# State-space rounds of a hybrid encoder: the step-weighted inputs made by ScalarE head by head, GpSimd making only the rows of the end states

## What is computed

```
acs  = cumsum(dt * A)                       # within a chunk of 128
xdt  = x * dt                               # the inputs weighted with the step size
Lm   = exp(acs[t] - acs[s]) for s <= t
y_diag = (C B^T * Lm) @ xdt                 # within a chunk
states = B^T @ (exp(acs_end - acs) * xdt)   # what a chunk adds to the state
prev   = scan of states over the chunks
y      = y_diag + (C @ prev) * exp(acs)
```

## Time and profile before

| | |
|---|---|
| median of 3 runs | 2319.83 us (2319.46 to 2322.78) |
| profiled execution | 2323.43 us, its span 2321.9 us |
| mean granted TensorE clock | 0.990 |
| busy: PE, DVE, ACT, POOL | 97%, 63%, 44%, 16% |
| state-space rounds | about 630 to 980 us of the span |
| `xdt` on POOL (L2349) | 48 instructions, 37.2 us, 801 ns in the mean |
| waits of POOL for PE ahead of `xdt` | 253.2 us |
| `rl` on ACT (L1287) | 192 instructions, 57.8 us |

### The profile page before, as it was taken

The page is one execution under the profiler, slowest core; times in us unless marked ns, Lnnn a source line. Parts: engine busy times, 40 slices in busy tenths (PEclk is TensorE's granted clock), DMA queues, the critical chain, the costliest instruction groups (busy, mean ns, idle before and its releaser), DMA issues.

```text
span 2321.9 us, 36382 instructions
## 1 busy us (share of the span) xinstructions
PE 2259.2 (97%) x13148; PEld 2013.1 (87%) x13148; DVE 1462.5 (63%) x2345; ACT 1016.0 (44%) x1651; POOL 371.1 (16%) x257
## 2 busy tenths in 40 slices
PE   8999999998999999999999999999999999999997
PEld 7999999997877777888888888888888899899996
DVE  7677677678778888422555555542246677677677
ACT  6334243344444754632455655544235334243244
POOL 2000000000012202133333333322333000000000
PEclk9999999999999999999999999999999999999999
DMA  3221221213111111223111111111342221221211
GB/s 119 66 73 55 73 72 54 72 40 124 46 34 31 36 45 27 55 82 91 46 46 46 45 45 45 43 31 46 104 131 69 68 73 55 73 72 54 73 57 71
DMA packets 252289, 144.65 MB, mean 62 GB/s; under 512 B 5728, under 2 KB 248592, under 8 KB 252192
## 3 DMA queue, kind: packets, MB, share of 16 engines
q1 hardware_dynamic: 249072, 130.63, 20.1%
q0 software_dynamic: 2352, 12.58, 1.6%
q10 hardware_dynamic: 768, 0.13, 0.0%
HBM read 133.89 MB, written 9.44 MB: 62 GB/s over the span
## 4 chain that ended last, share of the span: by engine, by line
PE 83%; DVE 7%; issue 5%; ACT 3%; POOL 1%; ACTq 0%; DMA 0%; DVEq 0%; POOLq 0%; SPq 0%
PE slot L516 36%; PE aux L547 23%; PE slot L596 14%; PE aux L917 1%; PE aux L806 1%; PE aux L885 1%; PE aux L793 1%; PE aux L899 1%; PE aux L776 1%; POOL wlo L2279 1%; PE aux L910 1%; PE slot L683 1%; DVE ca L1926 1%; PE aux L874 1%; DVE prev L1953 0%
## 5 line engine op out<-in xcount | busy, mean ns | idle before, releaser
L2279 POOL TENSOR_TENSOR wlo<-raw,whi 128x1024 fp32r<-128x1024 f32 (+1 forms) x100 | 232.5, 2325 | 1030.4 <-ACT whi L990 1030.3
L516 PE MATMUL slot<-xh,whi 128*128 128x256 f32 (+1 forms) x1360 | 364.1, 349 | 5.6 <-DVE gate L1584 2.2
L516 PE MATMUL slot<-xh,wlo 128*128 128x256 f32 (+1 forms) x1360 | 351.7, 340 | 0.0
L516 PE MATMUL slot<-xl,whi 128*128 128x256 f32 (+1 forms) x1360 | 350.7, 340 | 0.0
L516 PEld LDWEIGHTS slot<-xh,whi 128*128 128x128 f32 x1360 | 250.5, 188 | 45.4 <-issue 10.6
L516 PEld LDWEIGHTS slot<-xh,wlo 128*128 128x128 f32 x1360 | 256.1, 188 | 30.2
L516 PEld LDWEIGHTS slot<-xl,whi 128*128 128x128 f32 x1360 | 256.1, 189 | 29.9
L547 PE MATMUL aux<-th,whi 128*128 128x392 f32 (+1 forms) x640 | 220.7, 345 | 9.0 <-ACT work L1094 5.2
L1068 ACT ACTIVATE whi<-work 128x512 fp32r<-128x512 f32 x220 | 135.7, 626 | 198.9 <-DVE work L1642 105.1
L547 PE MATMUL aux<-tl,whi 128*128 128x392 f32 (+1 forms) x640 | 216.5, 338 | 0.0
L547 PE MATMUL aux<-th,wlo 128*128 128x392 f32 (+1 forms) x640 | 215.8, 337 | 0.0
(11 more groups left out here) (338 smaller groups left out, 4361.1 us busy)
## 6 DMA issues: line engine op xcount, KB each, us to landing
raw<-in_w_in SPq DMA_DIRECT2D x81, 512.0 KB, 3.9
raw<-in_ffn_w_gate_up SPq DMA_DIRECT2D x48, 512.0 KB, 4.3
work<-in_ffn_w_gate_up SPq DMA_DIRECT2D x40, 512.0 KB, 4.7
raw<-in_ffn_w_down SPq DMA_DIRECT2D x80, 256.0 KB, 3.1
raw<-in_ssd_w_proj SPq DMA_DIRECT2D x8, 512.0 KB, 3.8
raw<-in_hg_w_proj SPq DMA_DIRECT2D x8, 512.0 KB, 3.9
raw<-in_w_out SPq DMA_DIRECT2D x8, 512.0 KB, 3.9
h_spill<-h POOLq DMA_DIRECT2D x1, 3072.0 KB, 10.9
```

Of the source, the lines that this page charges most:

```text
L516: mm = pe.matmul(slot[b][:, PC + u:PC + v], w[b][:, t, :], x[:, t, u + off:v + off], start=(t == 0 and p == 0 and q == 0), stop=(t == k - ...
L2279: pool.tensor_tensor(wlo[s % 2][:, 0:k, :], raw[s % 2][:, 0:k, :], whi[s % 2][:, 0:k, :].bitcast(F32), ALU.subtract).then_inc(w_lo, 1)
```

## The change

`steps` is taken out of GpSimd's program. ScalarE gets `inputs(k, G)`, called right behind `decays(k, G)` in every step of the loop and of the last group: for a unit four instructions, one for each head, 128x64, a copy with the per-partition scale `gdt[:, c, d, h]`. The wait for `y_mm` and the count of `xdt_ok` go with them. In the loop GpSimd waits until all 12 inputs of the group are made and then makes the state inputs of the next group as before.

```diff
--- before.py
+++ after.py
@@ -1287,6 +1287,16 @@
                         ins = act.activation(m_s["rl"][u % 3][:, h, :], incl[d][:, :], ACT.Copy, scale=m_s["gal"][:, c, d, h:h + 1])
                     ins.then_inc(rl_ok, 1)
 
+            def inputs(k, G):
+
+                for u in S_STEPS[k][0]:
+                    c, d = S_UNITS[u]
+                    wait(act, y_mm, 4, Y_STEP[c - 2] if c >= 2 else 0, G)
+                    for h in range(HPG):
+                        ins = act.activation(m_s["xdt"][c % 2][d][:, PD * h:PD * (h + 1)], m_s["xbt"][:, c + 2, PD * h:PD * (h + 1)],
+                                             ACT.Copy, scale=m_s["gdt"][:, c, d, h:h + 1])
+                    ins.then_inc(xdt_ok, 1)
+
             def ssd_step(k, G):
                 for u in S_STEPS[k][0]:
                     wait(act, seg_mm, 2 * NC, u + 1, G)
@@ -1315,6 +1325,7 @@
                 for k in range(4):
                     ssd_split(k, N)
                     decays(k, G)
+                    inputs(k, G)
                     if k:
                         convolved(k - 1, N)
                     ssd_read(k, N)
@@ -1346,6 +1357,7 @@
             for k in range(5):
                 split(J_PA + 1 + k)
                 decays(k, last)
+                inputs(k, last)
                 pa_gate(k)
                 ssd_step(k, last)
             split(J_PA + 6)
@@ -2341,23 +2353,11 @@
                     pool.tensor_tensor(h4(xws[n][0:k, :]), h4(m_s["xbt"][0:k, q, 0:2 * P]),
                                        m_s["gw_t"][0:k, m, d, :].unsqueeze(2).broadcast_to([k, HPG, PD]), ALU.mult).then_inc(xw_ok, 1)
 
-            def steps(k, G):
-
-                for u in S_STEPS[k][0]:
-                    c, d = S_UNITS[u]
-                    wait(pool, y_mm, 4, Y_STEP[c - 2] if c >= 2 else 0, G)
-                    pool.tensor_tensor(h4(m_s["xdt"][c % 2][d][:, :]), h4(m_s["xbt"][:, c + 2, 0:2 * P]),
-                                       m_s["gdt"][:, c, d, :].unsqueeze(2).broadcast_to([P, HPG, PD]), ALU.mult).then_inc(xdt_ok, 1)
-
             ssd_weighted((0, None))
             with pool.Fori(0, GROUPS - 1) as g:
                 G, N = (0, g), (1, g)
-                for k in range(4):
-                    steps(k, G)
+                wait(pool, xdt_ok, 2 * NC, 2 * NC, G)
                 ssd_weighted(N)
-            last = (GROUPS - 1, None)
-            for k in range(4):
-                steps(k, last)
             for t in range(6, KT + 1):
                 low(J_PA + t)
             with pool.Fori(0, KT // 2) as i:
```

## The result

The changed kernel takes 2390.93 us (median of 6 runs, 2389.09 to 2398.02) against 2320.09 us for the kernel before: a ratio of 1.031 (95% interval 1.0295 to 1.0328), 71 us more. The forecast was 2391. The profiled execution took 2390.42 us, its span is 2388.9.

A forecast was written before the change was run, and what follows sets the result against it. PE, busy 97%, was taken to bound the kernel. Three loop rounds of 15.5 us (46.5), clock 20 and last group 5 made 71.5 us more, a median of 2391 us; range 2362 to 2411.

The forecast's parts named there:

- y1 to y2: Loop round, end of PE's output products of step 1 to step 2: 17.67 us against 13.5 before, 4.2 late.
- y2 to y3: Loop round, end of PE's output products of step 2 to step 3: 16.93 us against 12.5, 4.4 late.
- y3 to job 4: Loop round, end of step 3's output products to PE's projection job 4: 14.89 us against 8.02, 6.9 late.
- The price of an input: One 128x64 scaled copy on ScalarE: 0.24 us from start to start, bounds 0.15 and 0.29.
- Step 0 costs nothing: Step 0's twelve inputs, 2.9 us, fit into ScalarE's 13.25 us of idle time and wait for nothing new.
- The clock: PE's clock drops after three idle stretches per loop round: 2.2 us each, 6.6 a round, 20 in all.
- The last group: Group without convolution: y1 to y2 15.3 us, 2.0 late; y2 to y3 14.6, 3.0 late; 5.0 in sum.
- Rival (a): VectorE, undisturbed by GpSimd, gets faster: 3 us gained, 2316.8; chance 2%, plus 1% for its second form.
- long form: VectorE's subtraction, blocked by GpSimd's burst, is on the path: 10 us more gained, 2307; chance 1%.
- (b): In the loop rounds the waits cost what was forecast, but PE's clock holds: 2371 us; chance 14%.
- (c): PE's clock stays low much longer after idle stretches: 31.7 us a loop round, 2420 us; chance 8%.
- (d): ScalarE's queue is empty and its order immaterial, so no change: 2319.8 us; chance 2%.

The follow-up runs named there:

- e8: Changed kernel with matrix products nobody reads placed in PE's idle stretches of each loop round; 2379.0 us.
- e2: Kernel before, with ScalarE made to wait for y_mm where the change has its inputs, GpSimd still making them; 2358.8 us.
- e1: Changed kernel with each step's inputs moved behind that step's exponentials, same instructions and waits; 2346.5 us.
- e3: Changed kernel with four pairs of xdt buffers instead of two, so no input waits for outputs of its own step; 2335.7 us.
- e5: Changed kernel with each input cut into two of 32 columns, 384 instructions instead of 192; 2410.9 us.
- e7: Kernel before, with only step 0's inputs moved to ScalarE, the rest staying on GpSimd; 2321.0 us, ratio 1.0002.
- e4: Kernel before, with GpSimd making the inputs of units 4 to 11 only 4 columns wide; 2318.2 us, ratio 0.9988.
- e6: Changed kernel with the inputs spread: step 0's in idle time, steps 1 and 2's behind the next decays, step 3's behind its exponentials; 2339.0 us.

## Why the prediction was right, step by step

- **The chains at full clock.** e8 is the forecast's sum without the clock. y1 to y2: 17.67 forecast, 18.0 measured; y2 to y3: 16.93 and 17.2; y3 to job 4: 14.89 and 14.9. A loop round: 15.5 us late forecast, 50.2 - 34.0 = 16.2 measured. The steps were read from rows of the kernel before and added in the order in which each releases the next; e2, e1 and e3 show that it is the place of the wait that makes the chain.
- **The price of an input,** 0.24 us: 0.24. By e5 half the width costs 0.21 us ((5.20 - 0.31) / 23), as the slope has it, and the count on the path holds in the sum (19 expected, 20 measured).
- **Step 0 costs nothing:** shown by e7.
- **The clock:** forecast 6.6 us a round and 20 in all, measured 3.5, 5.6, 5.9 and 15.0. The right mechanism, sized a third above what was measured. Its term was mis-sized in the first round above all: against e8, its three stretches lost 1.1, 1.2 and 1.2 us, those of group 1 lost 2.2, 1.9 and 1.6, where 2.2 were forecast for each.
- **The last group:** forecast 15.3 and 14.6, measured 15.61 and 14.84; 5.0 against 5.6 in sum.
- The total was hit more exactly than its terms: 46.5 + 20 + 5.0 = 71.5 forecast, 48.6 + 15.0 + 5.6 = 69.2 in the trace, and 70.8 between the medians. The 5 us too many of the clock and the 2.7 too few of the other two partly cancel; that the median came out on the forecast to a tenth of a us is luck.
- **Rival (a)** has its mechanism but not its price: VectorE did become undisturbed in every step, and that is worth 2.4 us (e4) where nothing else changes, 3 being the forecast. Its long form is right about the blocking and not about the time: the subtraction went from 8.08 to 3.74 us in the change and 5.79 in e7, and no time came of it. The rule of the Trainium skill behind it (page "SBUF — State Buffer", section "Who interferes with whom") is that such instructions of VectorE and GpSimd contend, and that one fully blocks the other. The trace agrees for the subtraction, which takes 1.22 us alone, and not for the convolution's accumulations, which were only slowed (4.32 to 4.79 us for four).
- **Table loads:** one takes 1.28 us and the SiLU starts 1.29 after it (791.68 to 792.97), so the trace again does not show the 2.7 us that the Trainium skill (page "ScalarE: Activation LUTs", section "Rules for kernel authors") budgets.
- **Rivals (b), (c) and (d)** are out. (b), that the clock holds: it was 0.82 to 0.86, and e8 gets 12 us back. (c) had 31.7 us for a loop round, measured were 19.7 to 22.1. (d) had no change.

What the forecast did not say, and the runs show, is that wait and work cannot be priced each by itself and added: 38 us for the wait alone and 15 for the work alone, 71 for both. What stands behind the wait has to be counted with it. At full clock, as an estimate, the bare wait is 29 us (e2) and the inputs behind it, (28 x 3 + 20) x 0.24, are 25; the table has 48.6 + 5.6 = 54.2, and the clock's 15 come on top. And moving the wait away does not bring back the kernel before, since ScalarE's step is then full (e1, e6). No version with all inputs on ScalarE equalled the kernel before, the nearest being e3 with 15 us more; e7, with those of step 0 alone, equals it.

## What to carry to other kernels

Before work is moved to an engine that is idle half of the time, look at what it has to wait for and what is queued behind it there. In an in-order queue a wait that cost nothing on one engine delays everything behind it on the other, and the price is the whole chain from the wait to the next thing that the bound engine needs, with the moved work as one link of it. The test for free room is not the busy share of the span but the engine's own work in the stretch concerned: ScalarE, 44% busy over the span, was busy for 10.4 of 13.5 us from y1 to y2 and 11.1 of 12.5 us from y2 to y3 in the kernel before, and 2.9 us more filled its step (e1).

## What the runs showed of the hardware

- A PE that waits costs twice: 3.5 to 5.9 us a round went to the granted clock after idle stretches, and useless products in them made the kernel 12 us faster.
- Waits of PE of 2.3 to 5.4 us ahead of the transposes went with a granted clock of 0.75 to 0.76 from y3 to job 4 of group 1 in e1, e2, e3 and e6, where the kernel before has 1.00.
- Whether a short wait of PE brings a dip does not follow from its length alone. In e2 PE waited 2.1 us ahead of the segment products in every loop round; the stretches around these waits had 1.00 in group 0 and 0.89 to 0.90 in groups 1 and 2. In the last group, waits of 0.7 and 1.6 us left the clock at 1.00 in the changed kernel and went with two dips in e8, some 4 us apart. What decides it is not shown.
- VectorE's subtraction of 128x1024, 1.22 us alone, took 8.08 us beside a burst of fourteen instructions of GpSimd, 5.79 beside ten (e7) and 3.74 in the change, where it starts at the fifth of ten. In these three it ended 0.5 us ahead of the burst, whose last instruction then took 1.6 instead of 0.60 us: it got in once, ahead of the last. The convolution's accumulations were only slowed, from 4.32 to 4.79 us.
